# A two-layer decoder step on one Trainium2 core: weights and inputs laid out by the host, the conditioning accumulated over eight weight units and turned by VectorE, and the second layer's 24 conditioning units placed in the RWKV stage

## The reference

```python
def modulation(c, w_mod, b_mod):
    m = jax.nn.silu(c) @ w_mod + b_mod          # (9, 1024) @ (1024, 6144), for each layer
    return jnp.split(m[:, None, :], 6, axis=-1)

def trunk(x, c, conv_st, shift_st, wkv_st, w):
    for layer in range(DEPTH):
        sh1, sc1, g1, sh2, sc2, g2 = modulation(c, w['w_mod'][layer], w['b_mod'][layer])
        h = rmsnorm(x, ng[0]) * (1.0 + sc1) + sh1
        if layer % 2 == 0:
            y, nc, ns, nw = mixer_ab(h, ...)    # proj = h @ ab_w_in; conv and RWKV; @ ab_w_out
        else:
            y, v = gmlp_mixer(h, ...)
        x = x + g1 * rmsnorm(y, ng[1])
        h = rmsnorm(x, ng[2]) * (1.0 + sc2) + sh2
        x = x + g2 * rmsnorm(moe(h, ...), ng[3])
```

## Time and profile before

| | before |
|---|---|
| median of 3 runs (us) | 1762.97 (1759.73 to 1768.82) |
| the profiled execution, its time (us) | 1767.1 |
| its span, first to last instruction (us) | 1765.2 |
| PE busy | 1642.4 us, 93% |
| DVE, ACT, POOL busy | 672.8, 297.6, 204.5 us |
| mean granted TensorE clock | 0.955 of full speed |
| read from HBM | 533.36 MB |

### The profile page before, as it was taken

How to read it: one execution, slowest core, us unless ns; L and a number is a source line. 1 busy time by engine, 2 the same in 40 slices (tenths; PEclk the granted TensorE clock), 3 DMA queues, 4 the chain that set the end, 5 groups by cost and what they waited for, 6 DMA issues and landing times.

```text
span 1765.2 us, 28987 instructions
## 1 busy us (share of the span) xinstructions
PE 1642.4 (93%) x10816; PEld 1207.0 (68%) x10816; DVE 672.8 (38%) x1605; ACT 297.6 (17%) x603; POOL 204.5 (12%) x211
## 2 busy tenths in 40 slices
PE   6999998977999999999999979889999999999993
PEld 4777877876866666666666658876666666666662
DVE  2105565664333333333333433252333333333333
ACT  1012210002211111111111122131111111111111
POOL 1200079700100000000000000010000000000000
PEclk8889998898899999999999989989999999999996
DMA  9987772233399999999999373227999999999930
GB/s 298 262 260 240 242 241 97 72 121 145 117 366 404 406 411 405 401 401 406 399 401 406 127 292 120 100 95 307 406 401 411 408 407 402 401 411 402 397 157 25
DMA packets 144231, 519.48 MB, mean 294 GB/s; under 512 B 14917, under 2 KB 85827, under 8 KB 94130
## 3 DMA queue, kind: packets, MB, share of 16 engines
q1 hardware_dynamic: 131090, 493.13, 72.2%
q0 software_dynamic: 13088, 25.61, 4.6%
HBM read 533.36 MB, written 4.81 MB: 305 GB/s over the span
## 4 chain that ended last, share of the span: by engine, by line
PE 90%; DVE 5%; DMA 1%; issue 1%; ACT 1%; SPq 0%; POOL 0%; DVEq 0%; ACTq 0%
PE psum L657 83%; PE psum L660 7%; DMA ring<-in_ab_w_in 1%; DVE rstd L1415 1%; ACT arena L1210 1%; DMA arena<-in_x_sample 1%; DVE arena L1451 1%; DVE arena L1711 0%; DVE arena L1614 0%; SPq L402 0%; DVE arena L1610 0%; DVE arena L1611 0%; ACT rstd L1210 0%; DVE hT L1436 0%; DVE hT L1442 0%
## 5 line engine op out<-in xcount | busy, mean ns | idle before, releaser
L657 PE MATMUL psum<-ring,arena 128*64 128x256 f32 (+3 forms) x5360 | 720.6, 418 | 4.0 <-ACT arena L1210 2.4
L657 PEld LDWEIGHTS psum<-ring,arena 128*64 128x64 f32 (+1 forms) x5360 | 383.8, 139 | 297.0 <-issue 159.0
L1210 ACT ACTIVATE arena<-psum 128x512 f32<-128x512 f32 (+5 forms) x469 | 217.1, 498 | 1131.9 <-PE psum L660 590.7
L657 PE MATMUL psum<-arena 128*128 128x264 f32 (+2 forms) x1664 | 352.5, 367 | 14.8 <-DVE arena L1614 5.5
L657 PEld LDWEIGHTS psum<-arena 128*128 128x128 f32 (+1 forms) x1664 | 328.2, 281 | 45.0 <-issue 29.6
L1796 DVE TENSOR_TENSOR arena<-arena,psum 128x264 f32<-128x264 f32 x528 | 225.2, 429 | 45.0 <-PE psum L657 24.1
L657 PE MATMUL psum<-hT,ring 128*128 128x264 f32 x928 | 225.3, 403 | 17.7 <-DVE hT L1436 6.8
L657 PEld LDWEIGHTS psum<-hT,ring 128*128 128x128 f32 x928 | 188.3, 218 | 50.7 <-issue 12.0
L616 POOL DMA_INDIRECT arena<-h_rows,slot_idx x68 | 67.6, 994 | 995.5 <-DVE slot_idx L1785 979.6
L1823 DVE COPY arena<-psum 128x512 f32<-128x512 f32 x64 | 44.2, 691 | 274.6 <-PE psum L657 274.6
L660 PEld LDWEIGHTS psum<-K,arena 128*128 128x128 f32 (+5 forms) x994 | 114.0, 148 | 40.4 <-issue 27.7
(11 more groups left out here) (219 smaller groups left out, 713.2 us busy)
## 6 DMA issues: line engine op xcount, KB each, us to landing
ring<-in_moe_w_gate SPq DMA_DIRECT2D x128, 1024.0 KB, 8.6
ring<-in_moe_w_up SPq DMA_DIRECT2D x128, 1024.0 KB, 10.0
ring<-in_moe_w_down SPq DMA_DIRECT2D x128, 1024.0 KB, 6.7
ring<-in_w_mod SPq DMA_DIRECT2D x48, 1024.0 KB, 8.2
ring<-in_ab_w_in SPq DMA_DIRECT2D x13, 1024.0 KB, 8.2
ring<-in_gm_w_in SPq DMA_DIRECT2D x8, 1024.0 KB, 8.7
ring<-in_ab_w_out SPq DMA_DIRECT2D x4, 1024.0 KB, 6.1
ring<-in_gm_w_out SPq DMA_DIRECT2D x4, 1024.0 KB, 5.0
```

Source lines behind the costliest of these rows:

```text
L657: return nc.tensor.matmul(out, lhsT, rhs, start=start, stop=stop)
L1210: return nc.scalar.activation(out, in_, func, **kw)
```

## The change

The host lays out the large weights as whole units (each partition's 8 KB contiguous), turns x and c and the two states, and packs all small inputs into one array `small` that two transfers load. Turns of x, c and states on PE, and POOL's twenty transfers, go.

A w_mod unit now holds 128 inputs (one of the eight c tiles) for 2048 output columns. Eight units make a group g (two of the six vectors of a layer), and PE accumulates over the eight units in bank 6 or 7: per unit 4 matmuls of 512 columns instead of 8 of 256. DVE turns a group from PSUM in one 32x32-block transpose (L1412 of the changed kernel) and finishes both vectors (`mod_group`). ACT's copies and PE's turns go. Units 0 to 7 stand ahead of the projection, 8 to 23 in it (`MOD_AT`), 24 to 47, the second layer's, in the RWKV stage. The weights of both output projections are read without a step (`m * P:(m + 1) * P` for `m::DT`).

```diff
+MOD_AT = [8, 9, 10, 11, 13, 14, 15, 17, 18, 19, 21, 22, 23, 24]
...
+        "w_mod": tiles(w["w_mod"], 2, P, DT, 3, 2, 4, 32, DT).transpose(0, 3, 2, 1, 5, 4, 7, 6).reshape(NMOD, P, UNIT),
...
+        mod_loads(0, MOD_AT[0])
         for u in range(PROJT // 2):
             proj_unit.append(len(mix_units))
...
+            mix_units.append(("proj", ab_w_in[PROJ_ORDER[u]], DT))
+            mod_loads(MOD_AT[u], MOD_AT[u + 1])
+        mod_loads(MOD_AT[-1], NMOD)
...
-            load(ctok[0:1, :], c_prompt, "c_in")
-            load(ctok[1:NSEQ, :], c_sample, "c_in")
+            load(cin, c_T, "c_in")
+            load(xT[:, :, :], x_T, "x_in")
             load(K[:, 0:C_BLK], constants[:, 0:C_BLK], "const_in")
...
-                sp.dma_start(mix_view(n), mix_units[n][1]).then_inc(mload[n % MSLOTS], 16)
-
-            for n in range(2):
+                sp.dma_start(ring[:, n % MSLOTS, :], mix_units[n][1]).then_inc(mload[n % MSLOTS], 16)
+
+            for n in range(MSLOTS):
                 mix_load(n)
-            load(xtok[:, 0:2, :], x_prompt[0].rearrange("(t p) d -> p t d", p=P), "x_in")
...
+            load(small[:, 0:V_ROUTER], small_v[:, 0:V_ROUTER], "small_in")
+            for n in range(MSLOTS, 16):
                 mix_load(n)
...
+            def mod_units(a, b):
+
+                for u in range(a, b):
+                    g, c = u // DT, u % DT
                     arrived(mod_unit[u])
+                    if c == 0 and g >= 2:
+                        pe.wait_ge(S["mod_row"], g - 1)
                     w = mix_view(mod_unit[u])
...
+                    for j in range(4):
+                        last = mm(psum[32 * j:32 * j + 32, 6 + g % 2, :], cT[:, c, :], w[:, j, :], c == 0, c == DT - 1)
                     last.then_inc(S["mod_mm"], 1)
...
                 if pos % 2:
-                    for k in MOD_PROJ[pos // 2]:
-                        mod_half(k)
+                    mod_units(MOD_AT[pos // 2], MOD_AT[pos // 2 + 1])
                 beside_projection(pos)
...
-            pe.wait_ge(S["mod_set"], 8)
+            pe.wait_ge(S["mod_row"], 3)
             pe.wait_ge(S["tail_ready"], 1)
...
-            mod_half(17)
+            mod_units(24, 30)
...
-            mod_half(18)
-            mod_half(19)
+            mod_units(30, 34)
...
-            mod_half(20)
+            mod_units(34, 36)
             pe.wait_ge(S["xy0"], 2)
             for k in range(1, 6):
                 level_z(0, k)
                 if k <= 3:
                     gram_products(0, k + 1)
-                if k in (2, 4):
-                    mod_half(20 + k // 2)
+                mod_units(34 + 2 * k, 36 + 2 * k)
                 level_d(0, k)
             pe.wait_ge(S["xy"], 10)
             gram_products(1, 0)
             gram_products(1, 1)
-            mod_half(23)
-            mod_turn(11)
+            mod_units(46, 48)
...
+            def mod_group(g):
+
+                l = g // 3
+                dve.wait_ge(S["mod_mm"], DT * (g + 1))
+                V.transpose(modT.rearrange("p a c s -> p (a c s)"), psum[:, 6 + g % 2, :]).then_inc(S["mod_row"], 1)
+                dve.wait_ge(S["mod_row"], g + 1)
+                for a in range(2):
+                    part = g % 3 * 2 + a
+                    m, new, bias = mod[:, l, part], modT[:, a, :, 0:NSEQ], over(b_modT[:, l, part], NSEQ)
+                    if part % 3 == 0:
+                        last = V.tensor_tensor(m, new, bias, ALU.add)
+                    else:
+                        v(V.scalar_tensor_tensor(m, new, 2.0 - part % 3, bias, ALU.add, ALU.add))
+                        last = V.tensor_tensor(m, m, over(ngT[:, l, part // 3 * 2 + part % 3 - 1], NSEQ), ALU.mult)
+                    last.then_inc(S["mod_set"], 1)
+                dve.wait_ge(S["mod_set"], 2 * (g + 1))
+
+            dve.wait_ge(S["small_in"], 16)
+            mod_group(0)
             shift_samples(0, 0)
             shift_prompt(0, 0, range(DT))
-            mod_part(2)
...
+            mod_group(1)
+            dve.wait_ge(S["const2_in"], 16)
             dve.wait_ge(S["proj_sb"], PBT)
...
-            mod_part(7)
+            mod_group(2)
...
-            mod_part(8)
+            mod_group(3)
...
-                if k == 4:
-                    mod_part(10)
+                if k == 3:
+                    mod_group(4)
             gram_masks(1, 0)
             start_inverse(1)
-            mod_part(11)
+            mod_group(5)
             level_z(1, 1)
```

More of the change, by code:

```diff
@@ L43 @@
 EMH = float(np.exp(-0.5))
-NSMALL = 20
 UNIT = 2048
@@ L52 @@
 MAXR = -(-T // CAP)
-MOD_FIRST = 4
 PROJ_ORDER = [12, 6, 7, 8, 9, 10, 11, 0, 1, 4, 5, 2, 3]
 PROJ_TILE = [2 * u + i for u in PROJ_ORDER for i in range(2)]
-MOD_PROJ = [[MOD_FIRST + u] for u in range(13)]
-MOD_LATE = MOD_FIRST + sum(len(x) for x in MOD_PROJ)
+MOD_PART = 2 * DT
+NMOD = 6 * DT
+MOD_AT = [8, 9, 10, 11, 13, 14, 15, 17, 18, 19, 21, 22, 23, 24]
 NPAIR = NE // 2
@@ L82 @@
 NCONST = C_UPF + P
+V_BMOD, V_NG = 0, 12 * DT
+V_VEC = V_NG + 8 * DT
+V_GVEC = V_VEC + 54
+V_SHIFT = V_GVEC + 40
+V_CONV = V_SHIFT + PBT * NSA
+V_BROUT = V_CONV + 2 * QT * NSA
+V_ROUTER = V_BROUT + 2 * NE
+V_LORA = V_ROUTER + 2 * DT * NE
+V_GUP = V_LORA + DB
+NSMALL = V_GUP + DB
 def shape_constants():
@@ L101, in shape_constants @@
             c[:, C_LV0T:C_LV0T + P] = m.T
-    for j in range(4):
-        for s in range(NSEQ):
-            c[32 * j + s, C_S4 + s] = 1.0
     g = np.arange(8)
@@ L126, in build @@
+def build(nc, ins, outs):
+    (small_v, x_T, c_T, w_mod, ab_w_in, ab_w_out, gm_w_in, gm_w_out, state_conv, state_wkv, gm_w_s, gm_b_s,
+     moe_w_gate, moe_w_up, moe_w_down, moe_ws_gate, moe_ws_up, moe_ws_down, constants) = ins
     (y_prompt, y_sample, conv_p, conv_s, shift_p, shift_s, wkv_p, wkv_s, chunk_v_s) = outs
@@ L346, in build, with mod_loads @@
         mix_units, mod_unit, proj_unit = [], [], []
-        wm = w_mod.rearrange("l (p c) n -> l p c n", c=DT)
-        wi = ab_w_in[0].rearrange("(p c) n -> p c n", c=DT)
-        def half_units(k):
-            for u in (2 * k, 2 * k + 1):
+        def mod_loads(a, b):
+            for u in range(a, b):
                 mod_unit.append(len(mix_units))
-                mix_units.append(("mod", wm[u // 24, :, :, u % 24 * 256:(u % 24 + 1) * 256], DT))
-        for k in range(MOD_FIRST):
-            half_units(k)
+                mix_units.append(("mod", w_mod[u], 4))
@@ L691, in mod_half @@
-            def mod_half(k):
-                if k >= 1:
-                    pe.wait_ge(S["mod_row"], k)
-                if k % 2 == 0 and k not in (0, MOD_FIRST):
-                    mod_turn(k // 2 - 1)
-                for u in (2 * k, 2 * k + 1):
+            def mod_units(a, b):
+                for u in range(a, b):
+                    g, c = u // DT, u % DT
                     arrived(mod_unit[u])
+                    if c == 0 and g >= 2:
+                        pe.wait_ge(S["mod_row"], g - 1)
@@ L705, in _ @@
             pe.wait_ge(S["c_sb"], 1)
-            mod_half(0)
-            pe.wait_ge(S["x_in"], 32)
-            for t in range(2):
-                for c in range(DT):
-                    last = tr(psum[:, 2 * t + c // 4, (c % 4) * P:(c % 4 + 1) * P], xtok[:, t, c::DT])
-                last.then_inc(S["x_tr"], 1)
-            for c in range(DT):
-                last = tr(psum[:, 4, c * NSA:(c + 1) * NSA], xtok[0:NSA, 2, c::DT])
-            last.then_inc(S["x_tr"], 1)
-            mod_half(1)
+            mod_units(0, 2)
@@ L916, in _ @@
             level_d(1, 1)
-            pe.wait_ge(S["mod_set"], 12)
+            pe.wait_ge(S["mod_row"], 6)
             chunk_u(0)
@@ L1294, in _ @@
             last.then_inc(S["tok_sb"], 1)
-            for k in range(18, 24):
-                mod_rows(k)
             act.wait_ge(S["wkv_tr"], 1)
@@ L1891 @@
     arrays, ins, outs = {}, [], []
-    for name in _INS:
-        a = np.ascontiguousarray(inputs[name])
+    given = laid_out(inputs)
+    given.update((name, np.ascontiguousarray(inputs[name])) for name in _INS)
+    for name, a in given.items():
         arrays[f"in_{name}"] = a
```

251 lines of the change are left out of this document (82 added, 169 removed).

## The result

The changed kernel takes 1708.34 us (median of 4 runs, 1706.20 to 1714.90), the kernel before beside it 1763.22: a ratio of 0.9675, 95% interval 0.9635 to 0.9714. The forecast was 1697 with a range of 1680 to 1725. It named the right side and held the time, but counted on 66 us; the medians differ by 55, the profiled spans by 60.7 (1765.2 to 1704.5).

The account below looks back on a forecast made before the run. PE was taken as the bound (90% of the chain). Savings of 15.2 + 44.4 - 2.5 + 6.3 + 3 = 66.4 us took the profiled 1767.1 to 1700.7, with the median 4.1 lower: forecast 1697, range 1680 to 1725.

Parts of the forecast that it names:

- Start: Before the first projection tile: it starts at 34.9 instead of 50.06, saving 15.2 us.
- Projection: Projection stage, rebuilt from its units, small products and waits: 125.0 us instead of 169.35, saving 44.4.
- cross-check: Projection saving by what goes: six turns 22.2, ten units 9.4, small transposes 2.5, unit wait and half clock 10.3.
- the mixing: In the projection: `mod_group(1)` ahead of it on DVE makes it end 2.5 us later; 1.4 taken as PE's wait.
- To the first gram: Projection's end to first gram: the ring can't feed ten units, grams start after 20.5 us instead of 17.96; 2.5 lost.
- Inversion: Level loop at t = 0: 45.8 us instead of 52.06 with the new units in its levels, saving 6.3.
- PE covers some 3 us of it ... so 2 remain: Between levels 3 and 4: of 5 us for `mod_group(4)` on DVE, PE's products and units leave 2 uncovered.
- worst case by that rule: Groups 4 and 5: each of seven small DVE operations waits out a POOL instruction, 2.2 us; 8 us more, 1705.
- small operations stay blocked: Rival for groups 4 and 5: the seven small DVE operations take 12.3 us, 5 more in all, 1702; chance 0.10.
- the half clock: Rival: RWKV stage's PE work at half clock half of the time, 20 us more, 1717, up to 1737; chance 0.09.
- slower: Rival: unit stream below 217 GB/s misses the second inversion, kernel slower than before; 1790 at 200 GB/s; chance 0.03.
- slower units: Rival: units at 300 GB/s take 3.5 us; start loses 8.5, seven starved units 6.1; 1711; chance 0.13.

Follow-up runs that it names:

- the placing undone: Changed kernel with 32 w_mod units ahead of and in the projection and 16 in the RWKV stage, DVE's groups following: 1695.22 us, ratio 0.9584.

## Why the prediction was right, and where it missed

**Start.** 16.7 won, 15.2 forecast. The transpose took 0.72 (0.7 taken), the last unit was used at 27.50 (27.8), and its products took 1.07 (1.8). But the reason was half right at most. The 3.5 to 4 us for a unit in small pieces were read from means of slices; with the pieces back a unit takes 3.0, and the pieces are 5.9 of the 16.7; the other 10.8 lies in what stood between the units, where before's timeline has two turns (3.98 and 3.97 at 29.05 and 41.68) and the turning of x (4.66 at 16.56); that split was not tried.

**Projection.** 41.5 for 44.4; turns (26 to 29 with the half clock behind them), ten units, the wait for a unit and the small transposes make it up, much as the prediction's cross-check has it. The sentence "slow small pieces made the wait" is not borne out: with small pieces back (and ten units fewer than before) the projection has no such wait. The mis-sized term is the mixing: 1.4 were taken for a wait that took 1.9, and a tile at half clock behind it took 1.7 more; half of the delay is the constants' transfer, which the prediction did not name. What made the wait before was not tried. It falls on the seventh `ab_w_in` unit, the first that SP issues behind the second constants and the samples' state, and so does the 6.06 of the placing undone, which went when these were moved: a likeness and no proof. A unit took 1.0 instead of 0.94.

**To the first gram.** The step, that the ring can't feed ten units, was right and mis-sized: 4.9 instead of 2.5 lost. The ring waits are there (1.04, 1.22, 0.46, 2.05). The last unit's wait ends 21.0 us behind the projection (182.17) instead of 19.6, and its products then take 1.9 at 1.2 GHz instead of 1.0: that is nearly all of the 2.4. The transposes are slowed too (3.88 for 2.84), but lie ahead of that wait.

**Inversion.** The step that failed is "PE covers some 3 us of it ... so 2 remain", and the count of levels without half clock. Group 4 took 5.5 us (228.05 to 233.5) for the 5 taken, but PE waits 3.24 for it, and level 4 takes 11.9 (228.07 to 239.97) instead of the 10.05 of the sum. Level 1 started at half clock, 12.5 instead of 9.85, behind a wait of 5.20; before's own level 1, without a unit, had taken 10.5 (248.95 to 259.44) where later ones take 7.98, so that price stood in the trace. Levels 2 and 3 took 10.0 (9.85), level 5 0.35 less than its 6.2. Together they are the 4.6.

**The small operations beside GpSimd.** Two of group 4's took 2.19 and 2.38 (2.18 and 1.33 in the earlier trace rows), and without GpSimd 0.23. GpSimd's rows beside them:

```profile
228.53 2.36 POOL L587 TENSOR_TENSOR ring<-ring,arena 64x1024 f32<-64x1024 f32 x1
230.97 2.33 POOL L588 TENSOR_TENSOR arena<-ring,side_mem 64x1024 f32<-64x1024 f32 x1
```

DVE's two operations start just behind the start of one of these and end just behind its end (228.80 to 230.99, 231.02 to 233.40). The third starts at 233.32, ahead of GpSimd's next at 233.38, and takes 0.22. The Trainium skill, "SBUF — State Buffer" (section "SBUF: two separate sides"), names as the DVE operations that contend for the shared port's lock those with two SBUF inputs, against a GpSimd operation that reads SBUF, or in a two-port mode, and lets the one that starts first have it for the whole instruction. The trace agrees with both: the transpose out of PSUM stays at 0.72 and the masks out of PSUM at 0.69, and each operation that was held up ended with the GpSimd instruction that had started first. The prediction's worst case by that rule, in which each of seven small operations waits once, was too wide: group 5 took 0.41, 0.35, 0.22 and 0.23. The inverse's operations, with both operands in SBUF, meet GpSimd in the kernel before too (L1614 there takes 4.52 for two that take 1.28 where GpSimd is quiet) and gram to level stayed at 11.5 (8.34 without GpSimd's recurrence).

**Output projections.** 3 forecast; the rest of the span gave 4.2. The row taken, 19.51 for 80 records, is 0.244 each and not 0.24, by which 256 records give 3.9. Not tried by itself.

The rival "small operations stay blocked" and the half clock each came in part; "slower" and "slower units" did not: the stretch from 161 to 184 moved 384 GB/s, near the loops' 404.

## What to carry to other kernels

Price a removed operation together with the clock behind it, and in the place where it stood: six turns are 22 to 23 us of PE, and cost 14.0 more at half clock ahead of tiles, but 4.1 to 6.8 ahead of the halves where they had stood. Work that is moved into a stage where two engines alternate should stand where the one waits for the other anyway, and no more of it ahead of a product than the ring has loaded; here the same 24 units at other places were worth 13 us. A late start can move a DVE step under another engine's work on the same memory (the inverse's first operation took 2.06 with the grams at 22.9, 1.22 with them at 14), so look at what runs at the new time, not only at what was moved.

## What the runs showed of the hardware

- With no pause of PE at all, the granted clock fell to 0.50 in or behind each of the six turns put back (3.8 us of products with 9 moving columns and 128x128 weights); in the kernel before behind three of six.
- With pieces of 1 KB units of 1 MiB followed each other by 3.0 us at the start, with 8 KB by 2.5.
- While GpSimd works, DVE's operations with both operands in SBUF can go from 0.23 to 2.2 and from 1.22 to 2.1, and end with GpSimd's instruction; not all do (five of the seven small ones took 0.22 to 0.41). Those that read PSUM keep 0.69.
